# A matrix of gates built with one plain fp32 product per token in place of two fp32r products of rounded parts

## What is computed

```python
def block_fn(args):
    hx, ix, gx = args
    u = jnp.take(u_tab, ix, axis=0)
    act = jax.nn.gelu(jnp.einsum('chkd,cd->chk', u, hx), approximate=False)
    vv = jnp.take(v_tab, ix, axis=0)
    return jnp.einsum('chk,chkd->cd', gx * act, vv)
```

## Time and profile before

| | |
|---|---|
| median of 3 runs | 1829.7 us (1827.61 to 1834.57) |
| the profiled execution | 1831.82 us, of which the span from the first to the last instruction is 1828.9 us |
| mean granted TensorE clock | 0.879 |
| busy, TensorE matmul / weight load | 1437.2 us (79%) / 946.8 us (52%) |
| busy, VectorE / ScalarE / GpSimd | 1238.8 us (68%) / 420.2 us (23%) / 783.6 us (43%) |
| moved by DMA | 635.23 MB, mean 347 GB/s |

### The profile page before, as it was taken

How to read it: one execution, slowest core, us unless ns; L and a number is a source line. 1 busy time by engine, 2 the same in 40 slices (tenths; PEclk the granted TensorE clock), 3 DMA queues, 4 the chain that set the end, 5 groups by cost and what they waited for, 6 DMA issues and landing times.

```text
span 1828.9 us, 19105 instructions
## 1 busy us (share of the span) xinstructions
PE 1437.2 (79%) x7128; PEld 946.8 (52%) x7128; DVE 1238.8 (68%) x1829; ACT 420.2 (23%) x1246; POOL 783.6 (43%) x626
## 2 busy tenths in 40 slices
PE   2979999899899458889998876565688878788733
PEld 2559986888788336556676543332333323233200
DVE  5868787889889986665764698799745545544501
ACT  3004343854202253232330210110110101101020
POOL 1001011000122346554556677787766656556522
PEclk8989999999999769989999876666799998899877
DMA  9999998669788679998999999999999999999965
GB/s 340 386 389 405 400 356 320 245 241 379 268 316 310 196 283 397 349 369 340 397 366 409 346 366 353 349 371 337 363 404 407 400 370 372 377 419 415 363 228 191
DMA packets 148646, 635.23 MB, mean 347 GB/s; under 512 B 31516, under 2 KB 35794, under 8 KB 84050
## 3 DMA queue, kind: packets, MB, share of 16 engines
q0 software_dynamic: 82976, 446.76, 63.4%
q1 hardware_dynamic: 65580, 187.28, 26.8%
HBM read 789.15 MB, written 2.10 MB: 433 GB/s over the span
## 4 chain that ended last, share of the span: by engine, by line
PE 45%; DMA 27%; DVE 14%; POOL 7%; issue 5%; ACT 2%; DVEq 1%; SPq 1%; POOLq 0%; ACTq 0%
DMA v_rows<-in_peer_v,expert_rows 22%; PE ps L1117 14%; PE ps L454 9%; PE ps L1019 5%; DVE u_rows L1930 5%; PE ps L1167 5%; POOL v_rows L757 5%; PE ps L862 4%; DVE first_acc L483 3%; PE ps L856 2%; POOL u_rows L757 2%; PE ps L1084 2%; DMA ada_first<-in_w_ada 2%; DMA dense_rows<-in_dense_u 1%; PE ps L331 1%
## 5 line engine op out<-in xcount | busy, mean ns | idle before, releaser
L1930 DVE SCALAR_TENSOR_TENSOR u_rows<-u_rows,h 128x2048 f32<-128x2048 f32 x256 | 584.0, 2292 | 360.8 <-DMA u_rows<-in_peer_u,expert 357.5
L757 POOL DMA_INDIRECT v_rows<-in_peer_v,expert_rows x252 | 373.7, 1483 | 343.7 <-PE ps L1117 272.9
L1117 PE MATMUL ps<-v_rows,diag 128*32 128x512 f32 x2016 | 300.9, 751 | 275.6 <-DMA v_rows<-in_peer_v,expert_rows 274.3
L757 POOL DMA_INDIRECT u_rows<-in_peer_u,expert x256 | 366.4, 1431 | 232.4 <-DVE u_rows L1930 141.1
L1117 PEld LDWEIGHTS ps<-v_rows,diag 128*32 128x32 f32 x2016 | 80.2, 134 | 469.0 <-issue 468.9
L454 PE MATMUL ps<-h2T,dense_rows 128*128 128x256 f32 x1152 | 257.2, 384 | 5.3 <-DMA dense_rows<-in_dense_u 5.3
L1167 PE MATMUL ps<-dense_rows,dense_weight 128*128 128x512 f32 x576 | 254.7, 600 | 5.5 <-DVE dense_sums L1995 5.5
L454 PEld LDWEIGHTS ps<-h2T,dense_rows 128*128 128x128 f32 x1152 | 219.8, 192 | 50.4 <-issue 14.3
L1167 PEld LDWEIGHTS ps<-dense_rows,dense_weight 128*128 128x128 f32 x576 | 108.4, 191 | 152.7 <-issue 151.2
L306 POOL DMA_DIRECT2D ada_late<-in_w_ada x61 | 32.3, 529 | 304.0 <-DVE ada_acc L320 261.1
L320 DVE SCALAR_TENSOR_TENSOR ada_acc<-ada_late,cact,ada_acc 128x2048 f32<-128x2048 f32 x57 | 133.9, 2349 | 16.4 <-DMA ada_late<-in_w_ada 15.2
(11 more groups left out here) (297 smaller groups left out, 1745.9 us busy)
## 6 DMA issues: line engine op xcount, KB each, us to landing
ada_late<-in_w_ada POOLq DMA_DIRECT2D x61, 1024.0 KB, 7.8
dense_rows<-in_dense_u SPq DMA_DIRECT2D x36, 1024.0 KB, 9.0
dense_rows<-in_dense_v SPq DMA_DIRECT2D x36, 1024.0 KB, 9.0
ada_first<-in_w_ada SPq DMA_DIRECT2D x64, 512.0 KB, 11.7
ring<-in_w_in SPq DMA_DIRECT2D x10, 2048.0 KB, 26.9
ring<-in_w_o SPq DMA_DIRECT2D x8, 2048.0 KB, 16.7
ring<-in_w_peer_q SPq DMA_DIRECT2D x8, 2048.0 KB, 13.0
opened<-in_w_in SPq DMA_DIRECT2D x8, 1024.0 KB, 13.0
```

What stands on the lines that cost most here:

```text
L757: nc.gpsimd.indirect_dma_start(buf[:, :], None, table, bass.IndirectOffsetOnAxis(ap=places, axis=0), bounds_check=last_sparse, oob_is_err= ...
L1117: ins = nc.tensor.matmul(ps[rows, k, :], diag[n % len(diag)][:, :], v_slot(n)[0][:, 512 * k:512 * k + 512], start=first, stop=last)
L1930: nc.vector.scalar_tensor_tensor(out=u_rows[b][:, :], in0=u_rows[b][:, :], scalar=1.0, in1=h2[:, q // H, :], op0=ALU.mult, op1=ALU.mult, a ...
```

## The change

slots_out copies the gates once, in float32; weight_high, weight_low, weight_parts and their two semaphores are gone. one_hot makes plain float32 one-hots and multiplies by the gates once. scattered makes one plain fp32 product for each token in place of two fp32r products. VectorE's wait for the copied slots, which stood in weight_parts one step ahead of the first batch of each tile of tokens, now stands in one_hot of that first batch.

```diff
-    low_hot = [at(f"low_hot{b}", B + 4 * b * KB, [P, BATCH, NK], F32R) for b in range(2)]
-    high_hot = [[at(f"high_hot{k}_{b}", B + 8 * KB + 1152 * (2 * k + b), [P, BATCH, DENSE], F32R) for b in range(2)] for k in range(2)]
+    low_hot = [at(f"low_hot{b}", B + 4 * b * KB, [P, BATCH, NK]) for b in range(2)]
+    high_hot = [at(f"high_hot{b}", B + 8 * KB + 1152 * b, [P, BATCH, DENSE]) for b in range(2)]
...
                     o = bank[:, DENSE * k:DENSE * k + DENSE]
-                    nc.tensor.matmul(o, low_hot[i % 2][:, k, :], high_hot[0][i % 2][:, k, :], start=True, stop=False)
-                    ins = nc.tensor.matmul(o, low_hot[i % 2][:, k, :], high_hot[1][i % 2][:, k, :], start=False, stop=True)
+                    ins = nc.tensor.matmul(o, low_hot[i % 2][:, k, :], high_hot[i % 2][:, k, :], start=True, stop=True)
...
-                nc.scalar.copy(slot_rows[:, :, :].rearrange("p k t -> p (k t)"), bank[:, 0:3 * P]).then_inc(slots_turned, 1)
-                empty(nc.scalar.copy(weight_high[:, :], bank[:, 2 * P:3 * P]), f"slots{t}")
+                ins = nc.scalar.copy(slot_rows[:, :, :].rearrange("p k t -> p (k t)"), bank[:, 0:3 * P])
+                empty(ins, f"slots{t}")
...
-            def weight_parts(t):
-                dve.wait_ge(slots_turned, t + 1)
-                copied(dve, f"slots{t}")
-                nc.vector.tensor_tensor(weight_low[:, :], slot_rows[:, 2, :], weight_high[:, :].bitcast(F32),
-                                        ALU.subtract).then_inc(weight_parted, 1)
-                dve.wait_ge(weight_parted, t + 1)
...
-                high, low = high_hot[0][i % 2], high_hot[1][i % 2]
-                step(nc.vector.tensor_tensor(low[:, :, :], row(iota128[:, SPARSE:NK], DENSE), column(slot_rows[:, 0, :], DENSE), ALU.is_equal))
+                hot = high_hot[i % 2][:, :, :]
+                if b == 0:
+                    copied(dve, f"slots{t}")
+                step(nc.vector.tensor_tensor(hot, row(iota128[:, SPARSE:NK], DENSE), column(slot_rows[:, 0, :], DENSE), ALU.is_equal))
                 nc.vector.tensor_tensor(low_hot[i % 2][:, :, :], row(iota128[:, :], NK), column(slot_rows[:, 1, :], NK), ALU.is_equal)
-                step(nc.vector.tensor_tensor(high[:, :, :], low[:, :, :].bitcast(F32), column(weight_high[:, :].bitcast(F32), DENSE), ALU.mult))
-                nc.vector.tensor_tensor(low[:, :, :], low[:, :, :].bitcast(F32), column(weight_low[:, :], DENSE),
-                                        ALU.mult).then_inc(one_hots, 1)
+                nc.vector.tensor_tensor(hot, hot, column(slot_rows[:, 2, :], DENSE), ALU.mult).then_inc(one_hots, 1)
...
-                for t in range(TT):
-                    if n == batch_key(BATCHES * t) - 1:
-                        weight_parts(t)
```

More of the change, by code:

```diff
@@ L158, in build @@
     dense_weight = [at("dense_weight0", B + 16 * KB, [P, 28, T]), at("dense_weight1", C + 16 * KB, [P, 8, T])]
-    low_hot = [at(f"low_hot{b}", B + 4 * b * KB, [P, BATCH, NK], F32R) for b in range(2)]
-    high_hot = [[at(f"high_hot{k}_{b}", B + 8 * KB + 1152 * (2 * k + b), [P, BATCH, DENSE], F32R) for b in range(2)] for k in range(2)]
+    low_hot = [at(f"low_hot{b}", B + 4 * b * KB, [P, BATCH, NK]) for b in range(2)]
+    high_hot = [at(f"high_hot{b}", B + 8 * KB + 1152 * b, [P, BATCH, DENSE]) for b in range(2)]
     slot_rows = at("slot_rows", B + 8 * KB + 4608, [P, 3, P])
-    weight_high = at("weight_high", B + 14 * KB, [P, P], F32R)
-    weight_low = at("weight_low", B + 14 * KB + 512, [P, P])
     dense_sums = at("dense_sums", B, [P, TT, 512])
@@ L553, in build @@
                  "weights_spread", "diagonal", "summed", "ident32_ready"))
-    slots_turned, weight_parted, one_hots, dense_used, dense_summed, dense_taken, dense_added = map(
-        nc_sem, ("slots_turned", "weight_parted", "one_hots", "dense_used", "dense_summed", "dense_taken", "dense_added"))
+    one_hots, dense_used, dense_summed, dense_taken, dense_added = map(
+        nc_sem, ("one_hots", "dense_used", "dense_summed", "dense_taken", "dense_added"))
     y_taken, y_added, y_squared, y_var, y_std, y_rstd, y_done, out_stored = map(
```

## The result

The changed kernel takes 1836.64 us (median of 20 runs, 1831.5 to 1849.6), the one before 1829.42 us (20 runs, 1819.64 to 1838.23). That is about 7 us more by the medians, where I forecast 3 us less. The measured ratio of the two kernels is 1.0050 (about 9 us), with a 95% interval from 1.0031 to 1.0068.

What follows compares the result with a forecast made beforehand. A ring of row products, gathers and transfers was taken to bound the batches; 2 to 3 us of VectorE's lead plus 0.5 us for a late batch gave 3 us less, 1826.7 us, range 1815 to 1837.

Steps and rivals of the forecast that it cites:

- TensorE's part: Products per token: still 512 MATMUL at steps of 0.113 and 0.21 us, so change 0, bounds 0 to 3.6 us.
- VectorE's part: Each batch loses one multiplication, 15.7 us in all; only five of them, 2.5 us, lie on the chain.
- the ring: From 1056 us: 32 row products, gathers of v_rows, transfer, next group; 17.0 us a turn for 4 slots, VectorE not in it.
- The moved wait: VectorE's wait for the slots moves behind dot 98; one_hot(0) starts 3.1 us sooner, row-product group at 1042.2 near 1040.4.
- the case that the prediction named last: The prediction is wrong if VectorE's lead in the first four batches multiplies along the ring or is lost in its first turn.
- Rival (b): Batches: gathers miss their place before VectorE's dots, three fit per 6.85 us cycle instead of four; 1839 us, chance 0.11.
- arbitrary phases: Argument against rival (b): randomly timed gathers would wait 0.57 us on VectorE's locks, near the 0.65 us mean seen.
- Rival (a): Batches, 1028 to 1305 us: GpSimd is the true bound, so VectorE's saving goes through, 14 us less, 1815.7 us; chance 0.18.
- Rival (c): TensorE: plain product dearer at 36 columns, or clock falls because TensorE does less; +14 us, 1844 us; chance 0.07.

Runs made afterwards that it cites:

- the locking filler: Changed kernel plus one unused 128x288 multiplication per batch on VectorE, both inputs in SBUF: 1828.8 us, ratio 0.9976 to the kernel before.
- the second traces: Both kernels measured and traced again, nothing altered: changed kernel 1838.88 us, ratio 1.0055; kernel before 1826.71 us, ratio 0.9984.

## Why the prediction was wrong, step by step

**TensorE's part** was right: 512 instructions, 1.98 and 3.60 us for 16, so nothing gained. The trace agrees with the rows from 1 and 128 columns that bounded it, and with the locking filler the plain product costs no time in the whole that could be told (0.9976, 0.9946 to 1.0005).

**VectorE's part**: the size was right (32 multiplications gone, 13.8 us less in all), and so was the statement that the ring does not pass through VectorE. The step that failed is the price of nothing that hung on it. I costed only what VectorE's saving could bring and called the rest hidden in its idle time. It was not neutral: the gathers, which are in the ring, take their time from VectorE's pattern. With 0.49 us less between two pairs of dots the mean gather went from 1.59 to 1.73 us, the turns grew, and the time from the 19th to the 36th group went up by 4.1 us (6.8 us between the second traces) where I had 2 to 3 us less. VectorE's idle time grew by 18.7 us and not by 12, since the ring slowed.

**The moved wait**: in the first pair of traces the 3.1 us at one_hot(0) came as worked out, and the group behind it stands 15.6 us after the 19th and not 17.1 us, a gain of 1.5 us against the 1.8 forecast. I took it for kept. The next turn, 17.5 against 14.8 us, ate it, which is the case that the prediction named last. But the second trace of the kernel before has 15.5 us for that first turn, without any moved wait, so a gain of 1.5 us is no more than the scatter between two traces of one kernel. With the multiplications left in place, the moved wait shows no clear gain either.

**Rival (b)** was the right one, and had the mechanism that the runs showed: the start 0.04 us ahead of the dot, the shift of 0.49 us, three gathers in a cycle of 6.85 us (6.86 measured). I gave it 0.11, because the mean wait in the gathers, 0.65 us, was near the 0.57 us of arbitrary phases. That was the wrong argument. A mean that looks random does not say that the phases are random: the phases follow from VectorE's queue, since a gather that is caught is released by the end of the dot, and so stands again in the same place a cycle later. The rows bear this out: in the kernel before, the gather behind a batch stands at the same 0.03 to 0.05 us ahead of the dot in over half of the batches. The count of long gathers would have been the right test; it doubled from 20 to 40. The sign that I had named for (b), a mean gather of 1.8 us and more, was set too high: it is 1.73 and 1.76. Its price I put at 9 to 10 us; the traces give 6.4 us for the stretch (5.5 for the changed kernel alone), the ratio about 9 us (0.5% of 1829) with an interval down to 6. That it comes so near is luck: it was 29 us of which I took a third by guess.

**Rival (a)** falls: the saving made the kernel slower, and with more work on VectorE (the locking filler) it was as fast as before. **Rival (c)** falls: between the 19th and the 36th group the granted clock is 0.68 and 0.69 after, 0.66 and 0.65 before, and a batch of products costs what it did. The clock is even a little higher with the plain product: 0.68 to 0.71 in its ten traces, 0.65 to 0.68 in the four with fp32r. Why, and what that is worth, no run here tells.

What stays open is the part of the loss that lies outside the stretch, if any: 7.2 us by the medians and 9 by the ratio, against 5.5 us between the two traces of each kernel there; the rest is too small to be told from the scatter of the runs. No kernel tried is clearly faster than the one before. The lowest ratios, 0.9976 twice, are within 0.1% of what the kernel before reads against itself.

## What to carry to other kernels

Before taking work from an engine that is "not on the path", ask which engine's instructions wait for its gaps. Where one engine issues transfers between the locks of another, lay the two queues side by side in the timeline, look how far each start stands ahead of the next lock, and work out whether the change moves the lock past it: a miss of about 0.1 us decided here over 6 us. If the margin is thin, the order or length of the work between the locks is worth an experiment with a filler, long and short, before the arithmetic itself is blamed or praised.

A second form of a product costs what its instructions cost, not what the source's calls do: count the records of a similar product first.

## What the runs showed of the hardware that I had not expected

A VectorE instruction that reads PSUM and one SBUF operand held no gather here. With the keys in PSUM, all 31 gathers that started inside the second comparison took 0.99 us, the one at 1054.07 among them. With both operands in SBUF, 26 of the 28 in the same place of the kernel before took 1.32 to 1.34 us. The page SBUF — State Buffer of the Trainium skill (Who interferes with whom) says the same of an instruction with at most one SBUF input, outside VectorE's two-port modes, and the trace agrees. What I had not expected is how sharply it acts: a gather that starts 0.08 us ahead of a dot lasts 0.99 us, and one that starts 0.09 us behind its start lasts 3.06.
